# Exchanging the halves of the attention queries by two transfers within on-chip memory instead of a product on TensorE

## The chip, the core and the metric

The kernel runs on one core of a Trainium2 chip, in one launch. The metric is device time in microseconds (us). The engines are TensorE (PE, matrix products into PSUM banks), VectorE (DVE), ScalarE (ACT), GpSimd (POOL) and SyncE, whose queue (SPq) issues the DMA transfers. Each runs its own list of instructions in order and waits for the others on semaphores.

## The reference

Two transformer layers over 512 tokens of width 1024, in float32: a gated linear attention with an MLP, and a hybrid layer that joins a gated delta rule with an attention in which every query looks at the 128 keys that an indexer picks. The change touches this attention: 8 query heads of 128, two key heads. Before the scores, the first 32 dimensions of every query are rotated by position:

```
def apply_partial_rope(t, cos, sin):
    half = cos.shape[-1]                                # 16 here
    x1, x2 = tf[..., :half], tf[..., half:2 * half]
    out = jnp.concatenate([x1 * c - x2 * s, x2 * c + x1 * s, tf[..., 2 * half:]], axis=-1)
...
a_q = apply_partial_rope(rms_norm_2(a_q..., q_norm_g), cos, sin)
a_k = apply_partial_rope(rms_norm_2(a_k..., k_norm_g), cos, sin)
s = q_block . k_selected * scale ;  p = softmax(s) ;  o = p . v
```

## The kernel before, in words

Activations are kept with features on the 128 partitions and the 512 tokens along a row. So the halves that the rotation exchanges are partitions 0 to 15 and 16 to 31, and no elementwise engine can read one partition into another. The kernel computes `src = src * cos + swap(src) * sin`, in four steps that belong to four functions. `pool_rope` (L1111, POOL) multiplies by the cosine table, which is 1 from partition 32 on. `pe_rope` (L1105, PE) multiplies by a 128x128 matrix `swap_a` that exchanges the halves and changes one sign, into bank `b[5]`. `dve_rope` (L1116, DVE) multiplies that bank by the sine table, which is 0 from partition 32 on (L1120), and adds both (L1123). Semaphores `rp_cc`, `rp_ps`, `rp_ss` and `rp_out` count these steps over all rotations: 0 to 4 are the indexer's, 5 and 6 the two keys', 7 to 14 the eight query heads'.

The attention stage comes after the input projections. It goes through the heads i = 0 to 7, with two buffers each for queries `aq` and scores `ms` (e = i % 2). For one head the chain is:

- DVE `queries(i)` (L1480): normalised query into `aq`, counted by `r_y`
- POOL, PE (`turn`) and DVE: the rotation
- PE `scores(i)` (L1419): 4 products of 128 queries each with the causal part of the keys
- DVE `scores(i)` (L1493, L1498): the mask is added, the row maximum taken
- ACT `exponentials(i)` (L1463), DVE `normal(i)` (L1503, L1507): the softmax
- PE `spread(i)` (L1429): ten transposes; ACT copies them to SBUF (L1472)
- PE `values(i)` (L1438), DVE `output(i)` (L1486): times the values, times the gate

The order on each engine is written out by hand. In the loop, PE does spread(i), turn(i+3), values(i), scores(i+2). DVE does rotation(i+3), output(i), normal(i+1), queries(i+4), scores(i+2). So head i+4's query is made at the end of turn i of the loop and rotated at the start of turn i+1. POOL has only the cosine products here.

SPq does nothing during the attention before. It has issued the first three weight panels of the next stage (the gated delta rule) through `load` (L201) and then waits for the end of the stage (L1609, `phase_done`), before it fetches the rows of gates that the next stage reads.

Of the kernel before, what the change touches and what calls it, by code (L numbers as in the profile page):

```python
# [19 lines left out]
ALU = mybir.AluOpType  # L20
# [3 lines left out]
P = 128  # L24
# [26 lines left out]
ATT_H, ATT_KV = 8, 2  # L51
# [12 lines left out]
def host_constants():  # L64

    j, i = np.meshgrid(np.arange(P), np.arange(P), indexing="ij")
    masks = [(j == i)]
    for lv in range(LEVELS):
        s = 1 << lv
        masks.append((j // (2 * s) == i // (2 * s)) & (j % (2 * s) < s) & (i % (2 * s) >= s))  # L70
    masks.append(j <= i)
    masks = np.stack(masks, 1).astype(np.float32)
    ident = np.eye(P, dtype=np.float32)

    def rope(seq, rot, width):
        inv = (np.float32(500000.0) ** (-np.arange(0, rot, 2, dtype=np.float32) / np.float32(rot))).astype(np.float32)
        ang = (np.arange(seq, dtype=np.float32)[:, None] * inv[None, :]).astype(np.float32)
        half = rot // 2
        c = np.ones((P, seq), np.float32)
        s = np.zeros((P, seq), np.float32)  # L80
        swap = np.zeros((P, P), np.float32)
        for b in range(0, P, width):
            for f in range(half):
                c[b + f] = c[b + half + f] = np.cos(ang[:, f])
                s[b + f] = s[b + half + f] = np.sin(ang[:, f])
                swap[b + half + f, b + f] = -1.0
                swap[b + f, b + half + f] = 1.0
        return c, s, swap

    ca, sa, pa = rope(SEQ, 32, P)  # L90
    ci, si, pi = rope(SEQ, 16, IDX_D)
    keep = np.ones((P, SEQ), np.float32)
    keep[:, ::P] = 0.0
    half = np.where(np.arange(P)[:, None, None] < CHUNK, masks[:, :, :CHUNK], masks[:, :, CHUNK:])
    square = np.concatenate([ident, masks.reshape(P, -1), pa, pi, half.reshape(P, -1)], axis=1)
    wide = np.stack([ca, sa, ci, si, keep], 0)
    return square, wide


def build(nc, t, out, const_square, const_wide, gb_rows):  # L100
    with ExitStack() as ctx:
# [37 lines left out]
        def take(*shape):  # L139

            n = int(np.prod(shape))
            v = arena[:, at[0]:at[0] + n]
            at[0] += n
            assert at[0] <= 22400, at[0]
            if len(shape) == 2:
                v = v.rearrange("p (a b) -> p a b", a=shape[0])
            if len(shape) == 3:
                v = v.rearrange("p (a b c) -> p a b c", a=shape[0], b=shape[1])
            return v
# [927 lines left out]
        av = take(2, SEQ)  # L1077
        gtmp = take(3, SEQ)
        lg = gtmp[:, 0:2]
        top8 = take(3, 8)  # L1080
        assert at[0] <= kept0, (at[0], kept0)
        off = [0, 128, 384, 768]
# [22 lines left out]
        def pe_rope(pe, c, src, swap):  # L1105

            if not (isinstance(c, int) and c == 0):
                pe.wait_ge(s["rp_ss"], c)
            pe.matmul(b[5][:], swap[:], src, start=True, stop=True).then_inc(s["rp_ps"], 1)  # L1109

        def pool_rope(pool, c, src, cos):  # L1111
            if not (isinstance(c, int) and c == 0):
# [294 lines left out]
        t_at = {0: (b[3], 0), 2: (g_bank[1], 0), 3: (g_bank[0], 0), 1: (g_bank[0], P)}  # L1407

        def pe_att(pe):
            def turn(i, e):  # L1410

                pe.wait_ge(s["r_y"], i + 3)
                pe_rope(pe, i + 7, aq[:, e], swap_a)

            def scores(i, e):
                pe.wait_ge(s["rp_out"], i + 8)
                for q in S_ORDER:
                    bk, o = s_at[q]
                    last = pe.matmul(bk[:, o:o + P * (q + 1)], aq[:, e, q * P:(q + 1) * P], ak[:, e, 0:P * (q + 1)],  # L1419
                                     start=True, stop=True)  # L1420
                    if q != 0:
                        last.then_inc(s["s_ps"], 1)

            def spread(i, e):
                pe.wait_ge(s["pn_r"], TT * i + TT)
                for k in K_ORDER:
                    bk, o = t_at[k]
                    for q in range(k, TT):
                        last = pe.transpose(bk[:, o + (q - k) * P:o + (q - k + 1) * P],  # L1429
                                            ms[e][:, off[q] + k * P:off[q] + (k + 1) * P], ident[:])  # L1430
                    if k != 3:
                        last.then_inc(s["pt_ps"], 1)

            def values(i, e):
                pe.wait_ge(s["att_done"], i + 1)
                for n, k in enumerate(K_ORDER):
                    pe.wait_ge(s["pt_sb"], TT * i + n + 1)
                    last = pe.matmul(b[4][:, k * P:SEQ], v_key[e][:, k, :], p_t[:, koff[k]:koff[k] + SEQ - k * P],  # L1438
                                     start=(n == 0), stop=(n == TT - 1), skip_group_check=True)
                last.then_inc(s["pv_ps"], 1)  # L1440

            turn(0, 0)
            scores(0, 0)
            turn(1, 1)
            pe.wait_ge(s["nm_r"], TT)
            scores(1, 1)
            turn(2, 0)
            for i in range(ATT_H):
                e = i % 2
                spread(i, e)  # L1450
                if i + 3 < ATT_H:
                    turn(i + 3, 1 - e)
                values(i, e)
                if i + 2 < ATT_H:
                    pe.wait_ge(s["nm_r"], TT * (i + 2))
                    scores(i + 2, e)
# [19 lines left out]
        def dve_att(dve):  # L1476
            def queries(i):
                h, e = i // 2 + HPK * (i % 2), i % 2
                dve.wait_ge(s["r_r"], h + 3)
                dve.scalar_tensor_tensor(aq[:, e], q_all[:, h], gains[:, G_QN:G_QN + 1], q_sq[:, h],  # L1480
                                         ALU.mult, ALU.mult).then_inc(s["r_y"], 1)

            def output(i):
                h = i // 2 + HPK * (i % 2)
                dve.wait_ge(s["pv_ps"], i + 1)
                dve.scalar_tensor_tensor(o_att[:, h], o_att[:, h], 1.0, b[4][:], ALU.add, ALU.mult).then_inc(s["att_done"], 1)  # L1486

            def scores(i, e):
                for n, q in enumerate(S_ORDER):
                    dve.wait_ge(s["s_ps"], (TT - 1) * i + (1, 2, 3, 3)[n])  # L1490
                    w = P * (q + 1)
                    bk, o = s_at[q]
                    dve.tensor_tensor_reduce(out=ms[e][:, off[q]:off[q] + w], in0=bk[:, o:o + w], in1=sel[:, off[q]:off[q] + w],  # L1493
                                             scale=1.0, scalar=NOT_CAUSAL, op0=ALU.add, op1=ALU.max,
                                             accum_out=n_max[:, 4 * e + q:4 * e + q + 1]).then_inc(s["nm_r"], 1)
                dve.wait_ge(s["nm_r"], TT * i + TT)
                nm = n_max[:, 4 * e:4 * e + 4]
                dve.tensor_scalar(nm, nm, -P ** -0.5, None, ALU.mult).then_inc(s["nms"], 1)  # L1498

            def normal(i, e):  # L1500
                dve.wait_ge(s["ex_a"], TT * i + TT)
                r = r_sum[:, 4 * e:4 * e + 4]
                dve.reciprocal(r, r).then_inc(s["rs_r"], 1)  # L1503
                dve.wait_ge(s["rs_r"], i + 1)
                for q in S_ORDER:
                    m = ms[e][:, off[q]:off[q] + P * (q + 1)]
                    dve.tensor_scalar(m, m, r_sum[:, 4 * e + q:4 * e + q + 1], None, ALU.mult).then_inc(s["pn_r"], 1)  # L1507

            queries(0)
            dve_rope(dve, 7, aq[:, 0], sa)  # L1510
            queries(1)
            scores(0, 0)
            dve_rope(dve, 8, aq[:, 1], sa)
            queries(2)
            scores(1, 1)
            dve_rope(dve, 9, aq[:, 0], sa)
            normal(0, 0)
            queries(3)
            for i in range(ATT_H):
                if i + 3 < ATT_H:  # L1520
                    dve_rope(dve, i + 10, aq[:, (i + 1) % 2], sa)
                output(i)
                if i + 1 < ATT_H:
                    normal(i + 1, (i + 1) % 2)
                if i + 4 < ATT_H:
                    dve.wait_ge(s["s_ps"], (TT - 1) * (i + 3))
                    queries(i + 4)
                if i + 2 < ATT_H:
                    scores(i + 2, i % 2)
# [62 lines left out]
        def sp_gdn(sp):  # L1592
# [3 lines left out]
            for p in range(PAIRS):  # L1596
                cols = [(QKV0 + 1024 * kind, e) for kind, e in CONVS] + [(Z0, 0), (GTA0, 0), (Z0, 1), (GTA0, 1)]
                for u, (c, e) in enumerate(cols):
                    c += P * (2 * p + e)
                    load(sp, gdn_panel(p, u), [(w[:, :, c:c + P], 0)])  # L1600
                    if u == 2:
                        if p == 0:
                            sp.wait_ge(s["phase_done"], 16)
# [666 lines left out]
```

## Time and profile before

| | |
|---|---|
| median of 3 runs | 1725.9 us (1725.84 to 1730.27) |
| profiled execution | 1724.63 us, span 1722.4 us |
| mean granted clock of TensorE | 0.98 of full speed |
| busy, share of the span | PE 95%, DVE 56%, ACT 40%, POOL 14% |
| chain that ended last, by engine | PE 77%, DVE 10%, issue 6%, ACT 4%, POOL 1%, DMA 1% |
| `pe_rope` (L1109) on that chain | 1% of the span |

"Busy" of PE counts a matmul from start to modelled end, and matmuls overlap, so it says little of how much room there is. The chain says more: it is followed back from the last instruction to what released each one. The attention stage takes a stretch of about 70 us, from 848 to 916 us of the span. In the timeline rows the columns are start in us, length in us, engine, line, operation, what is written and read, and how often; in brackets stands how long the engine was idle before it and who ended that. A PE row of x2 or x8 lumps neighbouring passes of the same line.

### The profile page before, as it was taken

Reading aid. Unit: us, or ns where it says so; the run is one execution under the profiler, and the core shown is the slowest. Engines: PE = TensorE matmul, PEld = TensorE weight load, DVE = VectorE, ACT = ScalarE, POOL = GpSimd, SP = SyncE. Lnnn points to the kernel's source line nnn. Section 1 sums busy time; section 2 is a strip of 40 time slices with the busy share of each in tenths; the row PEclk is TensorE's granted clock in tenths of the full one; section 3 lists DMA queues with packets and bytes.
Section 4 is the critical chain, followed back from the end, with each engine's and each line's share of the span. In section 5 each row is a group of like instructions: output and inputs, shape, how many; then the busy total and the mean of one; then the engine's idle time right before and its main releaser. Section 6 shows DMA issues by size and latency. Waiting matters only on the chain.

```text
span 1722.4 us, 24745 instructions
## 1 busy us (share of the span) xinstructions
PE 1630.3 (95%) x9418; PEld 1300.5 (76%) x9418; DVE 972.4 (56%) x1489; ACT 682.1 (40%) x1033; POOL 238.1 (14%) x220
## 2 busy tenths in 40 slices
PE   6999969999999996999899999999998999999998
PEld 3777757888888873667557887878787788888887
DVE  5545545444444456578385858576775544444443
ACT  6455533413232334233454535363453332323232
POOL 0233420000000031134210401304040000000000
PEclk8999989999999998999899999999999999999999
DMA  4222202333333332223203222131320232333333
GB/s 134 77 66 62 74 25 85 98 98 97 98 91 104 87 96 68 74 61 86 63 1 86 62 63 75 50 79 38 85 72 26 77 106 87 105 90 98 97 98 98
DMA packets 258157, 135.06 MB, mean 78 GB/s; under 512 B 10699, under 2 KB 254940, under 8 KB 258068
## 3 DMA queue, kind: packets, MB, share of 16 engines
q1 hardware_dynamic: 258068, 133.84, 27.6%
q8 instruction: 61, 1.00, 0.2%
q14 instruction: 28, 0.23, 0.0%
HBM read 131.64 MB, written 2.18 MB: 78 GB/s over the span
## 4 chain that ended last, share of the span: by engine, by line
PE 77%; DVE 10%; issue 6%; ACT 4%; POOL 1%; DMA 1%; SPq 0%; DVEq 0%; POOLq 0%; ACTq 0%; PEldq 0%
PE bank L229 18%; PE bank L231 18%; PE bank L230 18%; PE bank L1613 4%; PE bank L491 3%; PE bank L493 3%; PE bank L492 3%; DVE arena L1918 2%; DVE w_lo L213 2%; ACT w_hi L209 2%; PE bank L1419 1%; PE bank L1438 1%; PE bank L1629 1%; PE bank L1109 1%; PE bank L1666 1%
## 5 line engine op out<-in xcount | busy, mean ns | idle before, releaser
L229 PE MATMUL bank<-h_hi,w_hi 128*128 128x512 f32 x960 | 386.1, 402 | 22.6 <-DVE h_lo L1009 10.5
L230 PE MATMUL bank<-h_lo,w_hi 128*128 128x512 f32 x960 | 376.5, 392 | 0.0
L231 PE MATMUL bank<-h_hi,w_lo 128*128 128x512 f32 x960 | 376.3, 392 | 0.0
L213 DVE TENSOR_TENSOR w_lo<-raw,w_hi 128x1024 fp32r<-128x1024 f32 x218 | 276.4, 1268 | 119.9 <-ACT w_hi L209 117.9
L209 ACT CAST w_hi<-raw 128x1024 fp32r<-128x1024 f32 x234 | 245.2, 1048 | 240.9 <-PE bank L231 217.8
L229 PE MATMUL bank<-m_hi,w_hi 128*128 128x512 f32 x608 | 238.7, 393 | 7.0 <-DVE w_lo L213 6.6
L229 PEld LDWEIGHTS bank<-h_hi,w_hi 128*128 128x128 f32 x960 | 182.0, 190 | 78.0 <-issue 23.1
L230 PE MATMUL bank<-m_lo,w_hi 128*128 128x512 f32 x608 | 237.2, 390 | 0.0
L231 PE MATMUL bank<-m_hi,w_lo 128*128 128x512 f32 x608 | 237.1, 390 | 0.0
L230 PEld LDWEIGHTS bank<-h_lo,w_hi 128*128 128x128 f32 x960 | 182.2, 190 | 40.1 <-issue 3.7
L231 PEld LDWEIGHTS bank<-h_hi,w_lo 128*128 128x128 f32 x960 | 181.9, 189 | 38.5
L229 PEld LDWEIGHTS bank<-m_hi,w_hi 128*128 128x128 f32 x608 | 114.5, 188 | 33.5 <-issue 6.9
L231 PEld LDWEIGHTS bank<-m_hi,w_lo 128*128 128x128 f32 x608 | 114.4, 188 | 24.0
L230 PEld LDWEIGHTS bank<-m_lo,w_hi 128*128 128x128 f32 x608 | 114.6, 188 | 23.5
L945 DVE TENSOR_TENSOR arena<-bank,arena 128x512 f32<-128x512 f32 x64 | 44.3, 692 | 147.0 <-PE bank L231 147.0
L935 DVE TENSOR_TENSOR arena<-arena 128x512 f32<-128x512 f32 x64 | 44.3, 692 | 132.6 <-ACT arena L911 132.6
L491 PE MATMUL bank<-h_hi,w_hi 128*128 128x512 f32 x272 | 116.8, 429 | 0.0
L911 ACT ACTIVATE arena<-bank 128x512 f32<-128x512 f32 x64 | 38.5, 601 | 174.5 <-PE bank L231 174.5
L493 PE MATMUL bank<-h_hi,w_lo 128*128 128x512 f32 x272 | 106.6, 392 | 0.0
L492 PE MATMUL bank<-h_lo,w_hi 128*128 128x512 f32 x272 | 106.4, 391 | 0.0
L2117 POOL TENSOR_TENSOR arena<-arena,half_masks 128x256 f32<-128x256 f32 x48 | 43.8, 933 | 311.8 <-DVE arena L1982 311.7
L1613 PE MATMUL bank<-arena 64*64 64x64 f32 x1984 | 73.0, 220 | 7.1 <-DVE arena L2060 4.0
(272 smaller groups left out, 2035.7 us busy)
## 6 DMA issues: line engine op xcount, KB each, us to landing
raw<-in_l_w_ff SPq DMA_DIRECT2D x64, 512.0 KB, 4.0
raw<-in_w_in SPq DMA_DIRECT2D x64, 512.0 KB, 3.8
raw<-in_w_mlp_up SPq DMA_DIRECT2D x32, 512.0 KB, 4.0
raw<-in_w_mlp_down SPq DMA_DIRECT2D x32, 512.0 KB, 4.0
raw<-in_l_w_in SPq DMA_DIRECT2D x24, 512.0 KB, 3.8
raw<-in_l_w_out SPq DMA_DIRECT2D x8, 512.0 KB, 3.8
arena<-gb_rows SPq DMA_DIRECT2D x16, 256.0 KB, 4.5
raw<-in_w_out SPq DMA_DIRECT2D x8, 512.0 KB, 3.9
```

The lines of the kernel that those rows point to most:

```text
L209: act.copy(w_hi[q.par][:], raw[q.par][:]).then_inc(s["w_hi_ready"], 1)
L213: dve.tensor_tensor(w_lo[q.par][:], raw[q.par][:], w_hi[q.par][:].bitcast(F32), ALU.subtract).then_inc(s["w_ready"], 1)
L229: pe.matmul(g_bank[q.par][:], w_hi[q.par][:, k], hi[:, k], start=(k == 0), stop=False)
L230: pe.matmul(g_bank[q.par][:], w_hi[q.par][:, k], lo[:, k], start=False, stop=False)
L231: last = pe.matmul(g_bank[q.par][:], w_lo[q.par][:, k], hi[:, k], start=False, stop=(k == KT - 1))
L491: pe.matmul(g_bank[q.par][:], w_hi[q.par][:, k], hi[:, k], start=(k == 0), stop=False)
L492: pe.matmul(g_bank[q.par][:], w_hi[q.par][:, k], lo[:, k], start=False, stop=False)
L493: last = pe.matmul(g_bank[q.par][:], w_lo[q.par][:, k], hi[:, k], start=False, stop=(k == KT - 1))
L935: dve.tensor_tensor(sq[:, u % 2], rl[:, u % 2], rl[:, u % 2], ALU.mult).then_inc(s["sqr"], 1)
L945: dve.tensor_tensor(down[:, u % 2], g_bank[q.par][:], r_sqr, ALU.mult).then_inc(s["dn"], 1)
L1613: return pe.matmul(o, left, right, start=True, stop=True, skip_group_check=True)
L2117: pool.tensor_tensor(halves(a_lv[e][:, lv % 2]), a_tr[e], half_mask(lv + 1), ALU.mult).then_inc(s["al_r"], 1)
```

## The change

The eight query rotations no longer use PE. Once `queries(i)` is done, SPq issues two transfers of 16 partitions by 512 elements within SBUF, from `aq` into a buffer `turned` of 32 partitions, with the halves exchanged. DVE waits for both, multiplies `turned` by a sine table that now carries the sign, and adds, on partitions 0 to 31 alone; the others keep the query, on which the rotation does nothing. POOL's cosine product stays as it is, and the five indexer and two key rotations still use PE. `swap_a` loses its minus sign, since the table has it. `turned` lies in space that the indexer used earlier, two buffers; SPq waits for the product with the one before last (`rp_ss`) before it overwrites one.

```
-    ca, sa, pa = rope(SEQ, 32, P)
-    ci, si, pi = rope(SEQ, 16, IDX_D)
+    ca, sa, pa = rope(SEQ, 32, P, True)
+    ci, si, pi = rope(SEQ, 16, IDX_D, False)
...
+        turned, ROT = gtmp[0:32, 0:2], 32
...
+        def sp_turns(sp):
+            for i in range(ATT_H):
+                sp.wait_ge(s["r_y"], i + 3)
+                if i >= 2:
+                    sp.wait_ge(s["rp_ss"], i + 6)
+                for dst, src in ((0, ROT // 2), (ROT // 2, 0)):
+                    sp.dma_start(turned[dst:dst + ROT // 2, i % 2], aq[src:src + ROT // 2, i % 2]).then_inc(s["rp_ps"], 16)
+
+        def dve_turned(dve, i, src):
+            c = i + 7
+            dve.wait_ge(s["rp_ps"], 7 + 32 * (i + 1))
+            dve.wait_ge(s["rp_out"], c)
+            dve.tensor_tensor(rp_s[0:ROT], turned[:, i % 2], sa[0:ROT], ALU.mult).then_inc(s["rp_ss"], 1)
+            dve.wait_ge(s["rp_cc"], c + 1)
+            dve.wait_ge(s["rp_ss"], c + 1)
+            dve.tensor_tensor(src[0:ROT], rp_c[0:ROT], rp_s[0:ROT], ALU.add).then_inc(s["rp_out"], 1)
...
         def pe_att(pe):
-            def turn(i, e):
-
-                pe.wait_ge(s["r_y"], i + 3)
-                pe_rope(pe, i + 7, aq[:, e], swap_a)
...
-            turn(0, 0)
             scores(0, 0)
-            turn(1, 1)
             pe.wait_ge(s["nm_r"], TT)
             scores(1, 1)
-            turn(2, 0)
             for i in range(ATT_H):
                 e = i % 2
                 spread(i, e)
-                if i + 3 < ATT_H:
-                    turn(i + 3, 1 - e)
                 values(i, e)
...
             queries(0)
-            dve_rope(dve, 7, aq[:, 0], sa)
+            dve_turned(dve, 0, aq[:, 0])
...
                 if i + 3 < ATT_H:
-                    dve_rope(dve, i + 10, aq[:, (i + 1) % 2], sa)
+                    dve_turned(dve, i + 3, aq[:, (i + 1) % 2])
...
                     load(sp, gdn_panel(p, u), [(w[:, :, c:c + P], 0)])
+                    if p == 0 and u == 1:
+                        sp_turns(sp)
```

PE before, from the last row sum of the projections (L1214) to the values of head 0. L1109 is a turn, L1419 scores, L1429 spread, L1438 values:

```order
L1214 MATMUL bank<-q_sq,ones 128x512 x2
L1109 MATMUL bank<-arena,swap_a 128x512
L1419 MATMUL bank<-arena 128x512
L1419 MATMUL bank<-arena 128x256
L1419 MATMUL bank<-arena 128x128
L1419 MATMUL bank<-arena 128x384
L1109 MATMUL bank<-arena,swap_a 128x512
...
L1109 MATMUL bank<-arena,swap_a 128x512
L1429 MATMUL bank<-ident,arena 128x128 x10
L1109 MATMUL bank<-arena,swap_a 128x512
L1438 MATMUL bank<-arena 128x512
```

The same place on PE now. L1433 is scores, L1443 spread, L1452 values:

```order
L1233 MATMUL bank<-q_sq,ones 128x512 x2
L1433 MATMUL bank<-arena 128x512
L1433 MATMUL bank<-arena 128x256
L1433 MATMUL bank<-arena 128x128
L1433 MATMUL bank<-arena 128x384
...
L1443 MATMUL bank<-ident,arena 128x128 x10
L1452 MATMUL bank<-arena 128x512
```

Four turns lie within these rows before and none now; scores of head 0 is PE's first work of the stage.

SPq before, around the attention. L1595 writes the gate rows out, L201 loads panels, L1609 and L1610 fetch gate rows after the stage:

```order
L1595 DMA gb_rows<-arena 40x512
L201 DMA raw<-in_w_in 128x8x128 x3
L1609 DMA arena<-gb_rows 128x512
L1610 DMA arena<-gb_rows 128x512
L1609 DMA arena<-gb_rows 128x512
```

SPq now (L1604, L202, L1620 and L1621 are the same lines, and L1119 the new transfers):

```order
L1604 DMA gb_rows<-arena 40x512
L202 DMA raw<-in_w_in 128x8x128 x2
L1119 DMA arena<-arena 16x512 x16
L202 DMA raw<-in_w_in 128x8x128
L1620 DMA arena<-gb_rows 128x512
L1621 DMA arena<-gb_rows 128x512
```

The sixteen transfers stand between the second and the third panel load, so the third load is now issued after the last head's exchange.

## Rows read from the trace of the kernel before

**Rows 1.** Chain of waits in the loop: start us, us, what.
```profile
873.01 1.31 PE bank L1429 x10
874.32 0.86 PE bank L1109 x2
875.18 2.16 PE bank L1438 x8
...
879.53 1.31 PE bank L1429 x10
...
899.07 1.31 PE bank L1429 x10
...
905.06 0.98 PE bank L1429 x7
```

**Rows 2.** Windows: length, busy PE, PEld, DVE, ACT, POOL; PEclk, DMA share, GB/s.
```profile
843.00:866.50 23.50, 13.94 (x29) 5.75 (x27) 11.67 (x33) 11.21 (x28) 3.80 (x3) 0.78 0.08 23
866.50:899.07 32.57, 32.44 (x141) 20.36 (x141) 27.76 (x82) 16.23 (x52) 6.39 (x5) 1.00 0.00 1
```

**Rows 3.** Timeline, DVE and POOL, one turn of the loop.
```profile
879.53 0.75 DVE L1480 SCALAR_TENSOR_TENSOR arena<-q_all,gains,q_sq 128x512 f32<-128x512 f32 x1
880.45 1.28 POOL L1114 TENSOR_TENSOR arena<-arena 128x512 f32<-128x512 f32 x1 [5.23 <-DVE arena L1480]
882.04 0.69 DVE L1120 TENSOR_TENSOR arena<-bank,arena 128x512 f32<-128x512 f32 x1
...
883.90 0.69 DVE L1486 SCALAR_TENSOR_TENSOR arena<-arena,bank 128x512 f32<-128x512 f32 x1 [0.37 <-PE bank L1438]
...
886.05 0.75 DVE L1480 SCALAR_TENSOR_TENSOR arena<-q_all,gains,q_sq 128x512 f32<-128x512 f32 x1
```

**Rows 4.** DMA issues: KB each, median us from issue to landing.
```profile
ident<-const_square SPq DMA_DIRECT2D x1, 64.0 KB, 1.9
raw<-in_w_in SPq DMA_DIRECT2D x2, 64.0 KB, 2.6
raw<-in_w_in SPq DMA_DIRECT2D x64, 512.0 KB, 3.8
```

**Rows 5.** Timeline, SPq: two neighbouring small issues, and its last before the attention.
```profile
4.47 0.29 SPq L287 DMA_DIRECT2D arena<-in_norm_mix_g  x1
4.81 0.29 SPq L287 DMA_DIRECT2D arena<-in_norm_mlp_g  x1
...
829.75 13.36 SPq L201 DMA_DIRECT2D raw<-in_w_in  x3
```

**Rows 6.** Timeline, PE and DVE, the start of the attention stage.
```profile
848.44 2.07 PE L1109 MATMUL bank<-arena,swap_a 128*128 128x512 f32 x2 [2.56 <-DVE arena L1480]
850.62 0.69 DVE L1120 TENSOR_TENSOR arena<-bank,arena 128x512 f32<-128x512 f32 x1 [2.23 <-PE bank L1109]
852.16 4.64 PE L1419 MATMUL bank<-arena 128*128 128x512 f32 x8 [1.65 <-DVE arena L1123]
856.59 1.86 PE L1109 MATMUL bank<-arena,swap_a 128*128 128x512 f32 x2
857.65 0.17 DVE L1498 TENSOR_SCALAR arena<-arena 128x4 f32<-128x4 f32 x1
...
860.20 2.40 PE L1419 MATMUL bank<-arena 128*128 128x512 f32 x8 [1.74 <-DVE arena L1123]
...
863.44 0.17 DVE L1498 TENSOR_SCALAR arena<-arena 128x4 f32<-128x4 f32 x1
...
866.50 1.31 PE L1429 MATMUL bank<-ident,arena 128*128 128x128 f32 x10 [3.05 <-DVE arena L1507]
```

**Rows 7.** Timeline, PE, three matmuls elsewhere in the kernel, two of them after idle time.
```profile
257.89 0.79 PE L229 MATMUL bank<-m_hi,w_hi 128*128 128x512 f32 x1 [2.93 <-DVE w_lo L213]
...
261.00 0.39 PE L230 MATMUL bank<-m_lo,w_hi 128*128 128x512 f32 x1
...
1327.25 0.49 PE L229 MATMUL bank<-m_hi,w_hi 128*128 128x512 f32 x1 [3.08 <-DVE w_lo L213]
```

More of the change, by code:

```diff
@@ L73, in host_constants, with rope @@
     ident = np.eye(P, dtype=np.float32)
-    def rope(seq, rot, width):
+    def rope(seq, rot, width, signed):
         inv = (np.float32(500000.0) ** (-np.arange(0, rot, 2, dtype=np.float32) / np.float32(rot))).astype(np.float32)
@@ L84, in rope @@
                 c[b + f] = c[b + half + f] = np.cos(ang[:, f])
-                s[b + f] = s[b + half + f] = np.sin(ang[:, f])
-                swap[b + half + f, b + f] = -1.0
+                s[b + half + f] = np.sin(ang[:, f])
+                s[b + f] = -s[b + half + f] if signed else s[b + half + f]
+                swap[b + half + f, b + f] = 1.0 if signed else -1.0
                 swap[b + f, b + half + f] = 1.0
         return c, s, swap
-    ca, sa, pa = rope(SEQ, 32, P)
-    ci, si, pi = rope(SEQ, 16, IDX_D)
+    ca, sa, pa = rope(SEQ, 32, P, True)
+    ci, si, pi = rope(SEQ, 16, IDX_D, False)
     keep = np.ones((P, SEQ), np.float32)
@@ L1509, in dve_att @@
             queries(0)
-            dve_rope(dve, 7, aq[:, 0], sa)
+            dve_turned(dve, 0, aq[:, 0])
             queries(1)
             scores(0, 0)
-            dve_rope(dve, 8, aq[:, 1], sa)
+            dve_turned(dve, 1, aq[:, 1])
             queries(2)
             scores(1, 1)
-            dve_rope(dve, 9, aq[:, 0], sa)
+            dve_turned(dve, 2, aq[:, 0])
             normal(0, 0)
```

## The prediction, on record before the changed kernel ran

> **What bounds the kernel now.** Of the page I read first the chain that ended last: it is PE's almost throughout, and the rotation's line L1109 has 1% of it. Since that is an average over unlike stages, the next view is the chain of waits inside the attention. In the loop it is an unbroken run of PE work: spread 1.31 us, turn 0.86, values 2.16, scores 2.16, and the next spread starts 6.52 us after the last (873.01 to 879.53) [rows 1]. The windows agree: PE is busy 32.44 of 32.57 us there at full clock, DVE 27.76 [rows 2]. That looks as if each turn taken off PE gave 0.86 us back. Two more views say otherwise. Where the loop has no turn left (head 5), the distance between spreads is 5.99 us (899.07 to 905.06) [rows 1]: values then has to wait for ACT's copies of the transposes, which the turn had covered. So PE's side of the loop falls by 0.53 and not by 0.86. And DVE's timeline shows that it is idle for only 0.37 us of its turn of 6.52 us (879.53 to 886.05) [rows 3]. DVE needs 6.15 us for its own work, and the change takes no instruction from it. Hence with PE relieved DVE is the limit, and the most that a turn of the loop can give is 0.37 us.
>
> In the start of the stage nothing overlaps: DVE, PE and DVE hand head 0 and head 1 to each other, and PEclk averages 0.78 [rows 2]. Scores takes 4.64 us for head 0 and 2.40 us for head 1 [rows 6]: the same eight passes at 1.2 and at 2.4 GHz.
>
> **The change part by part.** Profile against its own time of 1724.6 us.
>
> *DVE.* The product with the sine now reads SBUF twice, on 32 partitions instead of 128. I keep 0.69 us for it: the row gives 0.69 with a PSUM operand [rows 3], and it is rows of 512 elements that run, not partitions. Bounds: 0 to 0.1 us off each. The Trainium skill ("VectorE: DVE Perf Modes", the section on the TRN2 errata) states a smaller fixed cost for SBUF sources than for PSUM, 58 cycles against 120; an estimate by that page would be 0.065 us less for each of the eight products, 0.3 us over the loop. No row here shows such a gain, and the sum does without it. POOL's cosine product ends at 881.73, before the sine product at 882.04 [rows 3], so the two don't meet.
>
> *The wait that is added.* DVE waits for both transfers. Nothing in the trace is a transfer within SBUF. The nearest row is the 64 KB load with nothing before it, 1.9 us from issue to landing; another kind of 64 KB load takes 2.6 us [rows 4]. The second transfer is issued after the first, 0.34 us later by two neighbouring small issues [rows 5]. A plain sum is 2.24 us; I take 2.1, nearest to the first row and a little off because there are 16 rows to move and not 128. Bounds: 1.6 us, if so small a transfer saves much of the fixed part, and 2.6 + 0.34 = 2.94 us. The Trainium skill ("DMA: Bandwidth & Descriptors", latency section) speaks of a fixed cost of about 2 us per DMA, whatever the size; with the second issue that page's estimate would be 2.3 us, 0.2 more than mine.
>
> What hides it in the loop: after the query of head i+4 (ends at 880.28) DVE does the mask and maxima of head i+2 and is ready for the rotation at 882.04, 1.76 us later [rows 3]. A landing after 2.1 us thus holds DVE for 0.34 us, and behind DVE's wait stand output, normal and the next query, so everything in the loop. DVE's turn becomes 6.15 + 0.34 = 6.49 us against 6.52: nothing gained. Four turns of the loop (those that rotate heads 4 to 7) depend on it: 0 at 2.1 us, -1.5 us where it lands within 1.76, +3.2 us at 2.94 (0.81 each). Head 3's rotation is before the loop's first output and has room: 0, or up to +0.3.
>
> *The start of the stage.* Head 0: turn took from 848.44 to the product at 850.62 [rows 6], 2.2 us at half clock; the transfers take 2.1: -0.1. Head 1: its turn sat behind scores 0 and ran at half clock until 858.45, while DVE was free at 857.82 (857.65 + 0.17) [rows 6]. Its transfers have long landed by then: -0.7 more. Head 2: DVE came from the maxima at 863.61 and was not kept waiting: 0. So head 1's scores start 0.8 us earlier.
>
> *TensorE's clock.* This is the part that the diff hides. Before, PE worked from 852.16 to 858.45 without a break, scores 0 and then a turn; head 1's scores at 860.20 ran at full clock [rows 6]. Then a turn of head 2 of about a microsecond stood in the wait before the spread at 866.50. Now scores 0 is alone, 4.6 us, and between scores 1 (ends at about 861.8) and spread 0 (about 865.7) PE has nothing: 3.9 us idle. Elsewhere in this trace a wait of 2.93 us was followed by a matmul of 0.79 us, at half clock, and one of 3.08 us by the same matmul at 0.49 us, full clock; about 3 us after the first, matmuls were at 0.39 again [rows 7]. So 3 us idle can go either way, and 3.9 us will most likely cost the clock. The Trainium skill ("TensorE: Matmul & The Clock Gate") puts it as "the default state is throttled, and activity releases the throttle"; the rows agree, and it speaks against removing work from an engine that waits.
>
> The price: at half clock PE does half its work until the clock is back, and with 3.2 to 4.4 us of that (about 3 us after a start elsewhere [rows 7], over 4 us in scores 0 [rows 6]) it loses 1.6 to 2.2 us, 1.9 in the middle, in spread 0, values 0 and scores 2, which all lie on the chain. Against this stand 0.8 us from the start, and 0.5 for head 3's turn, which no longer stands between spread 0 and values 0. So +0.6 us if only this happens. If scores 0 alone doesn't bring the clock back, scores 1 runs at 4.64 instead of 2.40 us and adds 2.2: +2.8 us. Which of the two depends on how the work falls; I take the middle, +1.7 us.
>
> *SPq.* The exchange puts 16 transfers between the second and third panel load. Before, the three loads were out by 843.11 [rows 5]. Now the third is issued after head 7's query, which is ready near 893, and takes 3.8 us [rows 4]; the next stage starts after 915. Cost 0, cover 18 us. SPq itself has nothing else to do. A transfer of 32 KB has the DMA engines to itself (DMA share 0.00 in the loop [rows 2]).
>
> Sum: 1724.6 + 1.7 + 0 = 1726.3 us. The profiled execution was 1.3 us quicker than the median of the runs (1725.9); on the median the sum is 1727.6. I predict 1727.0 us.
>
> **The rivals.**
> - *The clock holds.* Then the 0.8 us remain, and of head 3's turn 0.2, since with PE that early output 0 waits for DVE's own rotation of head 3, -1.0 us, or -2.5 us with landing inside 1.76 us: 1723.4 to 1724.9 us. For it: the row of 0.49 us after 3.08 us idle [rows 7]. Against: 3.9 us is longer.
> - *Transfers land late; slower than before.* The place is DVE's wait in the loop, its price 4 times what exceeds 2.13 us (1.76 + 0.37), plus what exceeds 2.2 us once at head 0 and up to 0.3 at head 3. At 2.94 us that is +3.2 + 0.7 + 0.3 = 4.2 us, and with the clock's 1.7 us 5.9: 1731.8 us. It is measurably slower from about 2.8 us on. For it: the 2.6 us row [rows 4]; against: those loads stand behind other loads.
> - *Every turn pays.* If PE's chain were all, the loop would go to 5.99 us, 5 turns by 0.53 and 0.8 from the start: -3.5 us, 1722.4 us. It needs DVE to have 0.53 us of room where it has 0.37 [rows 3], and landing within 1.6 us.
>
> **How the numbers follow.** Forecast (clock lost once or twice, landing near 2.1 us) 0.55; clock holds 0.22; late landing 0.13, of which a good half reaches beyond 0.3%; every turn pays 0.05; something else 0.05. 0.3%, 5.2 us, is about what a measurement of this kernel can tell from no change. Only late landing with a lost clock gets there: slower 0.10, faster 0.03, same 0.87. The forecast's own range is 1725.2 to 1729.0; the range that holds 8 in 10 is 1723.3 to 1730.9 us.
>
> **What would show it.** In the new profile: PE without L1109 after 800 us; DVE's sine product in the loop waiting for a DMA for about 0.3 us each time, and turns of 6.4 to 6.5 us; issue to landing near 1.75 us for one transfer; spread 0 longer than 1.31 us and PEclk at 0.5 around it. I am wrong if the turn falls to 6.2 or less, if the transfers hold DVE by a microsecond, or if the clock stays full from head 1 on. A difference outside the attention stage would speak against the whole account.

## The result and the profile after

The changed kernel takes 1729.15 us (median of 20 runs, 1726.62 to 1731.03), the kernel before 1726.27 us beside it (20 runs). The ratio is 1.0016, 95% interval 1.0009 to 1.0023: 2.8 us slower, which is less than 0.3% and more than nothing. The forecast was 1727.0 us, in a range of 1723.3 to 1730.9 us; the range of its own mechanism was 1725.2 to 1729.0 us, and the result lies just above that.

The profiled execution took 1729.18 us. This is its chain of waits through the attention stage (start us, us, what; L1119 is the exchange, L1125 the sine product, L1433 scores, L1443 spread, L1452 values, L1489 the query), beside [rows 1] and [rows 6]:

```profile
849.34 0.62 SPq L1119
850.00 1.99 DMA arena<-arena
852.01 0.69 DVE arena L1125
...
853.53 4.65 PE bank L1433 x8
...
860.70 4.62 PE bank L1433 x8
...
869.15 2.20 PE bank L1443 x10
871.36 2.95 PE bank L1452 x8
...
876.50 0.77 DVE arena L1489
877.28 0.51 SPq L1119
877.83 1.99 DMA arena<-arena
879.84 0.69 DVE arena L1125
...
883.30 0.67 DVE arena L1489
...
916.91 4.10 PE bank L1452 x8
```

The reader sees three things. PE is no longer in the chain of the loop: DVE, the issue on SPq and the transfer are, and a turn takes 6.71 us where it took 6.52. Scores of head 1 now takes 4.62 us where it took 2.40, and spread 0 takes 2.20 instead of 1.31. And values of head 7, far from any edited line, takes 4.10 us where 2.41 is normal. The last two are the same thing, the clock. Windows, with the columns of [rows 2], for the start, the loop and the end:

```profile
843.93:869.15 25.22, 11.55 (x22) 5.17 (x20) 11.54 (x33) 11.21 (x28) 3.80 (x3) 0.66 0.03 8
869.15:903.49 34.34, 30.78 (x130) 19.71 (x130) 27.33 (x82) 16.32 (x52) 6.37 (x5) 0.95 0.10 26
903.49:922.00 18.51, 15.15 (x63) 9.40 (x64) 8.42 (x32) 8.79 (x29) 0.00 (x0) 0.91 0.01 1
```

PEclk, the mean granted clock of TensorE in a window, was 0.78 and 1.00 in the first two [rows 2] and is 0.66 and 0.95.

I measure the stage from the start of the first query to the start of the last `output`, in every trace below. Before it is 67.3 us (847.63 to 914.92), after 72.5 us (848.56 to 921.03). The 5.2 us are: +1.7 up to the start of spread 0, +0.8 in the first turn of the loop (7.33 us instead of 6.51), +0.95 in the next four, +1.7 after spread 5, all of it values of head 7. A second trace of the changed kernel (below) shows the same 72.5 us.

Two of DVE's waits in this stage, summed (who, for whom: us in total, times, longest):

```profile
DVE arena L1495 <- PE bank L1452: 10.3, 4, 5.6
DVE arena L1125 <- DMA arena<-arena: 8.3, 6, 2.7
```

Six of the eight rotations find DVE waiting for a transfer. At head 0 it waits 2.70 us, at head 3, in the first turn of the loop, 2.59 us. The wait at head 3 is covered: `output` of head 0, behind it on DVE, has to wait for values of head 0 for another 0.53 us.

```profile
872.35 0.68 DVE L1125 TENSOR_TENSOR arena<-arena 32x512 f32<-32x512 f32 x1 [2.59 <-DMA arena<-arena]
...
874.34 0.69 DVE L1495 SCALAR_TENSOR_TENSOR arena<-arena,bank 128x512 f32<-128x512 f32 x1 [0.53 <-PE bank L1452]
```

In the four turns that rotate heads 4 to 7 it is 0.74 us each:

```profile
876.50 0.75 DVE L1489 SCALAR_TENSOR_TENSOR arena<-q_all,gains,q_sq 128x512 f32<-128x512 f32 x1
...
879.84 0.68 DVE L1125 TENSOR_TENSOR arena<-arena 32x512 f32<-32x512 f32 x1 [0.74 <-DMA arena<-arena]
880.62 0.68 DVE L1128 TENSOR_TENSOR arena<-arena 32x512 f32<-32x512 f32 x1
881.23 0.67 DVE L1495 SCALAR_TENSOR_TENSOR arena<-arena,bank 128x512 f32<-128x512 f32 x1
```

The 0.37 us that DVE waited for PE before `output` [rows 3] are gone, and 0.74 us for the DMA are in their place. From the end of the query (877.25) to the product it is 2.59 us.

### The profile page after: what moved, and what is told of

Its sections match the earlier page's. It is cut to its first block, busy times and chain, and to the rows that moved or that the text cites. A ratio compares the mean times of both kernels' runs of the same rounds, so it can differ in the third digit from the quotient of the medians.

```text
span 1727.4 us, 24727 instructions
## 1 busy us (share of the span) xinstructions
PE 1627.7 (94%) x9402; PEld 1299.6 (75%) x9402; DVE 972.0 (56%) x1489; ACT 682.0 (39%) x1033; POOL 238.2 (14%) x220
## 3 DMA queue, kind: packets, MB, share of 16 engines
HBM read 131.64 MB, written 2.18 MB: 77 GB/s over the span
## 4 chain that ended last, share of the span: by engine, by line
PE 75%; DVE 10%; issue 7%; ACT 5%; POOL 1%; DMA 1%; SPq 0%; DVEq 0%; PEldq 0%; POOLq 0%; ACTq 0%; PEld 0%
PE bank L230 18%; PE bank L232 18%; PE bank L231 18%; PE bank L1624 4%; PE bank L492 3%; PE bank L494 3%; PE bank L493 3%; DVE arena L1929 2%; DVE w_lo L214 2%; ACT w_hi L210 1%; PE bank L1640 1%; PE bank L1433 1%; PE bank L1677 1%; PE bank L507 1%; PE bank L1452 1%
```

## The experiments

All are on one core. The first figure is the median with its ratio to the kernel before on the same chip, then the stage and a turn of the loop from the trace. e1 to e4, e5 to e8 and e9 to e12 are three groups on three chips, with the kernel before at 1726.87, 1726.43 and 1726.05 us beside them, so the ratio is the fairer figure across groups. The trace is of one execution. Those of e9 and e11 are the slowest of their eleven runs (1726.51 and 1725.59 us): stage and turn can be read from them, the whole time not.

| kernel | median us | ratio (95%) | stage us | turn us |
|---|---|---|---|---|
| before | 1726.3 | | 67.3 | 6.52 |
| changed | 1729.15 | 1.0016 (1.0009 to 1.0023) | 72.5 | 6.71 |
| e1 products at the start | 1730.77 | 1.0023 (1.0014 to 1.0032) | 69.8 | 6.71 |
| e2 products everywhere | 1729.86 | 1.0021 (1.0012 to 1.0030) | 70.8 | 6.71 |
| e3 no transfers | 1725.97 | 0.9999 (0.9990 to 1.0008) | 66.5 | 6.35 |
| e4 rotation later | 1737.72 | 1.0073 (1.0060 to 1.0087) | 77.1 | 7.73 |
| e5 third query buffer | 1733.04 | 1.0037 (1.0023 to 1.0050) | 73.1 | 6.38 |
| e6 and normal(0) early | 1729.20 | 1.0013 (1.0004 to 1.0022) | 69.5 | 6.38 |
| e7 before, normal(0) early | 1728.87 | 1.0017 (1.0008 to 1.0026) | 67.0 | 6.52 |
| e8 e6 and products | 1727.02 | 1.0006 (0.9997 to 1.0015) | 66.3 | 6.38 |
| e9 changed, kept warm | 1723.36 | 0.9986 (0.9977 to 0.9995) | 65.6 | 6.71 |
| e10 before, kept warm | 1724.65 | 0.9997 (0.9988 to 1.0006) | 66.2 | 6.52 |
| e11 e6, kept warm | 1722.85 | 0.9982 (0.9973 to 0.9991) | 63.8 | 6.38 |
| e12 changed, one run | 1728.95 | | 72.5 | 6.71 |

**e1, e2: TensorE busy as before.** `fill(i)` has the place and the wait of the old turn, but reads data that doesn't change and writes a bank that nobody reads:

```
+            def fill(i):
+                pe.wait_ge(s["r_y"], i + 3)
+                pe.matmul(b[5][:], swap_a[:], q_all[:, 0], start=True, stop=True)
+            fill(0)
             scores(0, 0)
+            fill(1)
             scores(1, 1)
+            fill(2)
```

e2 also has `fill(i + 3)` between spread and values.

> The changed kernel, with three products put back on TensorE where the rotations of heads 0 to 2 stood. They read unchanging data, and nobody waits for the result. Theory A (clock and landing both cost): scores of head 1 back to about 2.4 us and spread of head 0 to 1.31 us, the loop's turn still 6.7 us; 1.5 to 2.5 us less than the changed kernel. Theory B (only the wait for the transfers costs): no less than the changed kernel. Theory C (the clock is all of it): equal to the kernel before.

> As above with such a product in all eight places, so that TensorE does what it did before, and only the way by which the exchanged halves arrive is changed. Theory A: the turn of the loop stays at 6.7 us, since DVE's wait sets it and TensorE's 0.86 us fit beside it; as the kernel with three products, within 0.5 us. Rival (TensorE still bounds the loop): the turn grows by 0.5 us or more, 2 us more in all.

PE's timeline of e1 (L1437 scores, L1431 the unused products, L1447 spread, L1456 values):

```profile
855.20 4.63 PE L1437 MATMUL bank<-arena 128*128 128x512 f32 x8 [2.09 <-DVE arena L1128]
859.63 1.67 PE L1431 MATMUL bank<-q_all,swap_a 128*128 128x512 f32 x2
862.38 2.40 PE L1437 MATMUL bank<-arena 128*128 128x512 f32 x8 [1.08 <-DVE arena L1128]
864.61 1.02 PE L1431 MATMUL bank<-q_all,swap_a 128*128 128x512 f32 x2
868.62 2.40 PE L1447 MATMUL bank<-ident,arena 128*128 128x128 f32 x10 [2.99 <-DVE arena L1523]
870.81 4.19 PE L1456 MATMUL bank<-arena 128*128 128x512 f32 x8
```

Scores of head 1 is back at 2.40 us, so the turns of heads 0 and 1 that the change removed were what had brought the clock back. That is shown for the two together; neither was put back alone. But spread 0 does not come back to 1.31; it takes 2.40. Before, PE waited 3.05 us there and kept the clock [rows 6]; here it waits 2.99 us and loses it. The stage is 2.7 us shorter than in the changed kernel: 2.2 us up to the start of spread 0, 1.7 in values of head 7, and 1.2 lost again in the first turn of the loop. The median is not lower: that part of my expectation failed. In the trace, 2.9 us are given back after the stage, where the clock falls at 1007.7 us and in the changed kernel does not. e2 answers the other question. With 0.86 us of PE work back in each turn, the turn stays at 6.71 us, so PE doesn't bound the changed loop and its relief there is worth nothing. (Its median is 0.9 us below e1's; I had expected 0.5 at most.)

**e3: no transfers.**

```
-                    if p == 0 and u == 1:
-                        sp_turns(sp)
...
-            dve.wait_ge(s["rp_ps"], 7 + 32 * (i + 1))
```

> The changed kernel without the sixteen transfers and the wait for them; the exchanged halves are then never filled in. Theory A: the turn of the loop falls from 6.7 to 6.15 us, DVE's own work, and head 0 starts 2.7 us sooner; the clock is still lost around spread 0; 4 to 6 us less than the changed kernel, 2 to 3 less than before. Rival (every turn pays, TensorE is the limit): the turn falls to 5.99 us.

It is 3.2 us less than the changed kernel by the medians, 2.9 by the ratios, and level with the kernel before, where I had expected 4 to 6 less and 2 to 3 below before. The stage is 6.0 us shorter, 1.7 of it because values of head 7 keeps the full clock. But the turn is 6.35 us, neither the 6.15 that I had put on DVE nor the 5.99 of PE. DVE's timeline of e3 shows a wait that I had not listed (L1506 the last step of the maxima, L1511 the first of `normal`, L1471 the exponentials on ACT):

```profile
889.76 0.17 DVE L1506 TENSOR_SCALAR arena<-arena 128x4 f32<-128x4 f32 x1
889.83 0.67 DVE L1124 TENSOR_TENSOR arena<-arena 32x512 f32<-32x512 f32 x1
890.61 0.68 DVE L1127 TENSOR_TENSOR arena<-arena 32x512 f32<-32x512 f32 x1
891.33 0.69 DVE L1494 SCALAR_TENSOR_TENSOR arena<-arena,bank 128x512 f32<-128x512 f32 x1
892.28 0.18 DVE L1511 RECIPROCAL arena<-arena 128x4 f32<-128x4 f32 x1 [0.26 <-ACT arena L1471]
```

After the maxima, ACT takes 2.3 us for the exponentials (889.96 to 892.25), and `normal` needs them. Rotation and output fit into that time on DVE, with 0.26 us to spare. So maxima, exponentials, normal, query, maxima is a ring of 6.35 us through two engines, in which the rotation costs nothing at all. In the changed kernel another ring is longer and sets the turn of 6.71 us, as its chain shows: query, issue, transfer, rotation, output, normal, query.

**e4: the rotation later.**

```
-                if i + 3 < ATT_H:
-                    dve_turned(dve, i + 3, aq[:, (i + 1) % 2])
                 output(i)
                 if i + 1 < ATT_H:
                     normal(i + 1, (i + 1) % 2)
+                if i + 3 < ATT_H:
+                    dve_turned(dve, i + 3, aq[:, (i + 1) % 2])
```

> The changed kernel, but DVE does the rotation of head i+3 after output(i) and normal(i+1) instead of before. The transfers then have 4 us instead of 1.85 to land. Theory A: no wait for a DMA in the loop, turn 6.15 to 6.2 us for 4 or 5 turns, clock at the start still lost: 2 to 2.5 us less than the changed kernel, about equal to the kernel before. Theory C (the clock is all of it): as the changed kernel, within 0.5 us.

The expectation was far off: no wait for a DMA is left, and the turn is 7.73 us. The timeline of e4 tells why (L1507 last of the maxima, L1495 output, L1472 exponentials, L1512 normal):

```profile
887.42 0.17 DVE L1507 TENSOR_SCALAR arena<-arena 128x4 f32<-128x4 f32 x1
887.62 0.69 DVE L1495 SCALAR_TENSOR_TENSOR arena<-arena,bank 128x512 f32<-128x512 f32 x1
...
889.95 0.18 DVE L1512 RECIPROCAL arena<-arena 128x4 f32<-128x4 f32 x1 [1.64 <-ACT arena L1472]
```

Without the rotation in it, DVE stands 1.64 us in the shadow of the exponentials, and the rotation is paid behind them. It confirms the ring of e3 and refutes the picture of a DVE that is busy with its own work.

**e5, e6, e8: the query out of the ring.** A third query buffer lets DVE make head i+4's query at the beginning of a turn, before the rotation of head i+3, so that a whole turn covers its transfers. (The two heads in flight have a semaphore each, since their transfers could land in either order.)

```
+        aqs = [aq[:, 0], aq[:, 1], gtmp[:, 2]]
...
             for i in range(ATT_H):
+                if i + 4 < ATT_H:
+                    dve.wait_ge(s["s_ps"], (TT - 1) * (i + 2))
+                    queries(i + 4)
                 if i + 3 < ATT_H:
+                    dve_turned(dve, i + 3, aqs[(i + 3) % 3])
                 output(i)
```

e6 also does `normal(0, 0)` before `scores(1, 1)` on DVE, and e8 adds `fill(0)` and `fill(1)`.

> The changed kernel with a third query buffer, so that each head's query is made one turn of the loop earlier, before the rotation of the head ahead of it. Theory A2 (the loop is a ring: scores, exponentials on ACT, normal, query; beside it DVE's wait for the transfers): with the query out of the ring and the landing covered by a whole turn, no wait for a DMA, the turn falls from 6.71 to 6.15 to 6.2 us (DVE's own work). With the clock at the start lost as in the changed kernel: 2 to 2.5 us less than that. Rival (landing doesn't matter, the ring alone does): the turn stays above 6.35 us.

> As e5, and DVE does normal(0) before the maxima of head 1, so that TensorE can go from scores of head 1 to spread of head 0 with no more than 1 us idle instead of 3.8. Theory A2: the clock doesn't fall a second time around spread of head 0; spread 0 starts 1.5 to 3 us sooner than in e5; another 2 us less. Rival (the clock doesn't matter): only the 1.5 us or less by which DVE's order is shorter.

> As e6, with unused products on TensorE where the rotations of heads 0 and 1 stood. Theory A2: the clock is back for the scores of head 1 (2.4 us instead of 4.6), so 1 to 2 us less than e6, and the mean granted clock is higher than e6's. Rival: no difference.

After the first turn of the loop no DMA wait is left in any of the three (in the first, at head 3, e6 and e8 still wait 0.55 us), and the turn is 6.38 us: 0.33 less than in the changed kernel, but not 6.15. The ring is not the reason, although the number would suit that rival: in e5's turn DVE has no wait at all. The first product of `normal`, 128x512, takes 0.87 us there instead of 0.49, because it meets POOL's cosine product, which now runs at another time (L1134 the cosine product, L1517 `normal`):

```profile
889.75 1.27 POOL L1134 TENSOR_TENSOR arena<-arena 128x512 f32<-128x512 f32 x1 [5.11 <-DVE arena L1129]
890.43 1.65 DVE L1517 TENSOR_SCALAR arena<-arena 128x512 f32<-128x512 f32 x4
```

In e3, where the two don't meet, the four products of `normal` take 1.27 us together and not 1.65:

```profile
892.50 1.27 DVE L1515 TENSOR_SCALAR arena<-arena 128x512 f32<-128x512 f32 x4
```

In e5 the first one ends about 0.28 us after POOL's product. The two overlap so in the three turns of 6.38 us of e5, e6 and e8, and in no turn of the kernel before or the changed one. Without these 0.38 us DVE's work would be 6.0 us; that was not tried.

The median of e5 is nevertheless 3.9 us higher than the changed kernel's. In the stage it is only 0.6 us: spread 0 starts 1.75 us later, since DVE makes a fourth query before it (0.67 us) and the first product of `normal` of head 0 takes 1.57 us beside POOL's instead of 0.49 (1.08 us), and the half clock lasts through spread 0 and values 0. Another 3.0 us stand behind the stage in its trace. From e5's chain:

```profile
860.90 4.62 PE bank L1434 x8
...
871.09 2.40 PE bank L1444 x10
873.48 3.73 PE bank L1453 x8
```

e6 takes the wait before spread 0 away and is 3.8 us lower than e5; the clock falls a second time all the same, at 869.4 us in values of head 0 (4.08 us), which I had expected it not to do. e8 brings the clock back for head 1 and is 2.2 us lower again, as expected. Of the three only e8 is level with the kernel before.

**e7: early normal alone.** The kernel before with the same two lines exchanged, as in e6.

> The kernel before, with normal(0) before the maxima of head 1 and nothing else changed. It tells how much of e6 has nothing to do with the transfers. Theory A2: the loop stays at 6.51 us (TensorE with its turns), the start gains 1 to 2 us against the kernel before. If e6 gains no more than this against before, the third buffer and the transfers bring nothing.

The expected gain of 1 to 2 us is not there: the stage is 0.3 us shorter, and the median is 2.4 us higher than before. Here too the first product of `normal` of head 0 meets POOL's and takes 1.24 us instead of 0.49, and the clock falls a second time, at 866.9 us. Its trace lost the clock outside the stage where the trace of before had not, at 1003 us. The same happens in e1, e3, e5, e6, e8, e10 and e11, between 1001 and 1010 us, and not in the changed kernel. The rest of the kernel (span less stage) varies from 1654.7 us (e12) to 1660.0 us (e11) over the traces, and the traces tell where. Part of it lies ahead of the stage, where no edit reaches: the first query starts at 847.6 us in the kernel before and between 848.1 and 850.2 in the changed one and e1 to e8. The other part lies behind it: from the last `output` to the end it is 806.4 us in both traces of the changed kernel, 807.5 in the kernel before, and 808.8 to 809.4 in the eight traces that lose the clock between 1001 and 1010 us. So against the trace of before, the changed kernel has 0.9 us more ahead of the stage, 5.2 more in it and 1.1 less behind it. That is why stage and median don't go together kernel by kernel.

**e9, e10, e11: TensorE kept busy in its waits.** `warm(n)` issues n unused products without a wait of their own:

```
+            pe.wait_ge(s["lg_r"], 24)
+            warm(3)
+            pe.wait_ge(s["r_y"], 3)
+            warm(4)
             scores(0, 0)
+            warm(2)
             scores(1, 1)
+            warm(3)
...
                 values(i, e)
+                if i == ATT_H - 2:
+                    warm(2)
```

This is e9. e10 has three before turn 0 and two behind it, and the two at the end; e11 is as e9 without the last three at the start, on the order of e6.

> The changed kernel with unused products on TensorE in the waits at the start of the attention (three before the first query is ready, four while its halves travel, two after scores of head 0, three after scores of head 1) and two after values of head 6. Clock theory: PEclk stays at 1.00 from 843 us to the end of the stage, scores of heads 0 and 1 take 2.4 us each instead of 4.6, spread of head 0 1.31; the stage gets about 6 us shorter than the changed kernel's 72.5 us, and the median falls by 4 to 6 us, 2 to 3 below before. Rival (alignment elsewhere decides): the stage gets shorter, but the rest of the kernel gives back more than half of it.

> The kernel before, with such products in its waits (three and two at the start, two after values of head 6). Clock theory: scores of head 0 at 2.4 us; the stage 2 to 3 us shorter than before's 67.3 us, the loop still 6.51 us. What e9 gains over this is what the transfers are worth without the clock; I expect e9 between 0.5 us shorter and 1 us longer.

> As e6 (third query buffer, normal(0) early) with unused products at the start (three, four, two) and two after values of head 6. Clock theory: full clock through the stage, loop 6.38 us, the stage 62 to 64 us against before's 67.3; the median 2.5 to 5 us below before and below the changed kernel, the only version that beats both. Rival as in e9.

PE's timeline of e9 at the start of the stage (L1431 the unused products, L1437 scores):

```profile
848.07 6.42 PE L1431 MATMUL bank<-q_all,swap_a 128*128 128x512 f32 x14
854.96 2.43 PE L1437 MATMUL bank<-arena 128*128 128x512 f32 x8 [0.47 <-DVE arena L1128]
857.23 1.88 PE L1431 MATMUL bank<-q_all,swap_a 128*128 128x512 f32 x4
859.93 2.40 PE L1437 MATMUL bank<-arena 128*128 128x512 f32 x8 [0.82 <-DVE arena L1128]
```

and its windows, start, loop and end:

```profile
846.00:866.50 20.50, 17.37 (x47) 7.67 (x46) 11.70 (x33) 10.93 (x28) 3.82 (x3) 1.00 0.04 10
866.50:900.00 33.50, 29.27 (x132) 18.54 (x130) 27.08 (x82) 16.22 (x52) 6.36 (x5) 1.00 0.11 27
900.00:916.20 16.20, 14.72 (x66) 8.91 (x64) 8.01 (x31) 8.57 (x28) 0.00 (x0) 1.00 0.00 1
```

The clock stays whole, scores of heads 0 and 1 take 2.4 us, and with nothing else changed the changed kernel falls from a ratio of 1.0016 to 0.9986, 5.2 us (5.8 by the medians): 0.14% below the kernel before, although its loop still turns at 6.71 us. So keeping the clock is enough to undo the loss. It doesn't show that the transfers are free: e3, which takes the transfers away and still loses the clock at heads 0 and 1, is level with the kernel before too. Either one alone undoes the loss. The trace of e9 also bears the rival out in part: against the trace of the changed kernel the stage is 6.9 us shorter and the rest 4.2 us longer, more than half. By the medians of eleven and twenty runs most of the gain stays.

e10 shows that the kernel before profits less (ratio 0.9997, its interval holds 1), and its stage is 1.1 us shorter where I had expected 2 to 3: it lost the clock at spread 0, where PE had its 3.05 us wait. e9 is 1.3 us below e10 by the medians, but their intervals overlap, and e10 lost the clock once, so what the transfers are worth at full clock stays open. e11 is the best of all by its median, 1722.85 us, although its clock fell once, at 868.9 us in values of head 0 (3.55 us). It beats both kernels; from e9 it is not told apart (the intervals overlap).

**e12: the changed kernel once more.**

> The changed kernel once more, for a second trace. If the clock meets this stage at the same place each time, scores of head 1 take 4.6 us again and the stage 72 to 73 us; if the late loss in values of head 7 was chance, it is absent and the stage is 70.8 us.

It took 1728.95 us. The chain of this second trace:

```profile
853.29 4.65 PE bank L1433 x8
...
860.47 4.62 PE bank L1433 x8
...
868.91 2.19 PE bank L1443 x10
871.10 2.96 PE bank L1452 x8
```

The stage is 72.5 us again, and values of head 7 is slow again (the clock fell at 917.0 us, as at 917.2 in the first). In two traces out of two these losses stand at the same place.

## Why the prediction was right, and where not

Step by step:

- *PE is not the limit of the loop once it is relieved.* Right, shown by e2 (PE's work back, turn unchanged).
- *DVE's own 6.15 us are the floor.* Wrong. The floor is 6.35 us, by the ring through ACT's exponentials (e3, and e4 by making it worse). I had read DVE's idle time in [rows 3] and not asked what DVE would wait for next. With the kernel's order of work the most a turn could give was 0.17 us, not 0.37. Nor was 6.15 us its own work: in the changed kernel's turn that is 5.97 us, 6.71 less the wait of 0.74.
- *Landing.* The term was undersized: 2.1 us from query to product, measured 2.59 (2.7 at head 0). The 1.99 us from issue to landing of one transfer is what [rows 4] had (1.9). The larger errors are the issue, 0.55 us from one to the next in the loop instead of the 0.34 us of [rows 5], and the 0.14 us that I took off the plain sum of 2.24 because there are only 16 rows to move: no row supported that, and no run shows it. It is more than half way to the rival of late landing. The turn came to 6.71 instead of 6.49 us, +0.95 us over four turns where I had 0. It is no more because two errors partly cancel: the landing is 0.49 us later, and the rest of the turn takes 4.12 us where 6.49 less 2.1 is 4.39. My own sign of being wrong, DVE held by a microsecond, does not show in the turns that count (0.74 us) and does show at head 3 (2.59 us), where it costs nothing.
- *Head 0 and head 1 at the start.* Head 0's transfers cost 0.45 us (3.45 us from the start of the query to the product, against 2.99) instead of giving 0.1. Head 1's product waited for nobody, as forecast, and its scores start 0.43 us sooner after the first query instead of 0.8.
- *The clock.* Right in place and mechanism: scores of head 1 at 4.62 us, and half clock again at spread 0 and values 0. Up to the spread of head 1 the profile shows +2.5 us, and the forecast's worse case, both losses at once, was +2.8. The 1.7 us that I put into the sum was the middle of two cases, and not what either would give. e1 and e9 show the cause by experiment.
- *The end of the stage.* Not foreseen: values of head 7 at half clock, 1.7 us, in both traces of the changed kernel. Between spread 7 and what comes before it, PE waits 2.18 us there as before; why the clock survives that before and not after was not isolated. The same loss is there in e4, e5, e6 and e8, and not in e1, e2, e3 and e7; e1 waits the same 2.18 us there and keeps the clock.
- *SPq and the third panel.* Right: it was issued at 898.6 us and nobody waited for it.

The sum was +1.7 us on the profile. The two profiles differ by 4.6 us (1724.63 to 1729.18), the medians by 2.9, because the profiled execution of before was one of its better ones. So the place and the kind of the loss were right and its size was not: the stage lost 5.2 us, three times the forecast. That 1727.0 us comes within 2.2 us of the result is in part luck: only 2.9 of the 5.2 us reach the medians. The 0.6 us between the sum of 1727.6 and the forecast has no reason given, and without it the forecast would have been nearer. Span and mean granted clock are known for every run of the changed kernel, and of the kernel before for the runs beside the experiments: beside e1 to e4 (29 runs) it has 0.979 and 1725.0 us in the middle, the changed one 0.976 and 1727.4. Of these runs of the kernel before, ten at 0.978 have 1725.6 us in the middle and two at 0.982 have 1720.5, 1.3 us per 0.001. At that rate 0.003 of clock are worth about 3.8 us, an estimate from few runs, but enough to cover the 2.4 us between the two spans.

What stays open is why the rest of the kernel takes up to 5 us more or less from one trace to another. The traces show where the clock falls in each case, not what would fix it in place.

## What to carry to other kernels

Before taking work from an engine that isn't the only limit, look at what keeps its clock: here the two products removed around scores of head 0 cost 2.2 us in scores of head 1, and fourteen unused products in the waits gave 5.2 us back by the ratios. Before moving an instruction out of a wait, find the ring: what DVE did between the maxima and `normal` was free, because ACT was computing for it. After moving one, see what it now meets: POOL's product cost `normal` 0.38 us a turn. And in an exchange of data by DMA count each issue as well as the landing: two transfers of 16 rows took 2.6 us from the end of the query to the product, 0.5 us of it because the second had to wait for the issue of the first.

## What the runs showed of the hardware

- A transfer of 16 partitions by 2 KB within SBUF lands 1.9 to 2.0 us after its issue, no sooner than 64 KB from device memory (1.9 us [rows 4]). Its issue occupies SPq for 0.51 to 0.62 us, against 0.37 us (median) for a panel of 512 KB. DMA issues of the changed kernel from 840 to 900 us:

```profile
arena<-arena SPq DMA_DIRECT2D x16, 32.0 KB, 2.0
raw<-in_w_in SPq DMA_DIRECT2D x1, 512.0 KB, 4.2
```

- The product on 32 partitions from SBUF takes 0.68 us, the one on 128 partitions from PSUM 0.69 [rows 3], and the addition before, on 128 partitions from SBUF (L1123), 0.69: neither the number of partitions nor the source made a difference of more than 0.01 us. The smaller fixed cost for SBUF sources that the prediction quoted from the Trainium skill ("VectorE: DVE Perf Modes", the section on the TRN2 errata) doesn't show here; the measurement decides.
- The clock meets this stage at nearly the same place in all eleven traces in which it falls at the start: 0.3 to 0.75 us after the start of the first query (before 848.03 us, changed 848.9, e1 850.7, e4 848.5, the latest e7 with 0.73). So which wait loses the clock repeats from trace to trace.
- Waits of 3.05 us (before, spread 0), 3.05 us (e10, spread 0) and 2.99 us (e1, spread 0) ended differently, the first at full clock, the others at half. The length of a wait alone doesn't tell; the work around it was not the same.
- A product of `normal` on DVE (TENSOR_SCALAR, 128x512, both sides in SBUF) that meets POOL's cosine product takes longer the more they overlap: 0.48 or 0.49 us alone in every trace, 0.87 us with an overlap of 0.59, 1.57 us with 1.26. In all 18 cases (e5, e6, e7, e8, e11) it ends 0.28 to 0.31 us after POOL's product. What holds it was not isolated.
